# Moving the rounded operands of a hybrid DeltaNet/MoBA block to other addresses in SBUF

## The reference, cut to what matters

```
h = rms_norm(x, norm_pre_w)
proj = h @ w_in                                   # 1024 x 10256
qkv_a, z_a, beta_a, dec_a, qkv_b, z_b, gate_logits = split(proj)
oa = gated_delta_rule(conv+silu+l2norm of qkv_a, beta, g)     # 8 heads of 128, chunks of 64
ya = rms_norm(oa, dn_onorm_w) * silu(z_a)
ob = moba_attention(qkv_b, rel_bias)              # 8 heads of 128; one block of 256: causal attention with a bias
yb = ob * silu(z_b)
gates = sigmoid(gate_logits + b_gate)             # two branches
merged = gates[0] * (ya @ w_branch[0]) + gates[1] * (yb @ w_branch[1])
out = x + rms_norm(merged @ w_out, norm_post_w)
```

## Time and profile before

| | |
|---|---|
| median of 3 runs | 357.66 us |
| the profiled execution | 357.55 us |
| its span (first to last instruction) | 355.8 us |
| TensorE matmuls busy | 347.6 us (98%), 2387 records |
| TensorE weight loads busy | 318.4 us (89%) |
| VectorE busy | 270.0 us (76%) |
| ScalarE busy | 218.8 us (62%) |
| GpSimd busy | 58.7 us (16%) |
| moved by DMA | 63.48 MB, mean 178 GB/s |
| granted clock of TensorE | 0.998 |

### The profile page before, as it was taken

One profiled execution on the slowest core, in us unless ns is written; L12 is line 12 of the kernel. 1 busy time (PEld: TensorE's weight loads), 2 busy tenths in 40 slices (PEclk: granted clock), 3 DMA queues, 4 the chain that ended last, 5 costly groups with the idle time before them and its releaser, 6 DMA issues.

```text
span 355.8 us, 6674 instructions
## 1 busy us (share of the span) xinstructions
PE 347.6 (98%) x2387; PEld 318.4 (89%) x2387; DVE 270.0 (76%) x551; ACT 218.8 (62%) x483; POOL 58.7 (16%) x114
## 2 busy tenths in 40 slices
PE   7999999999999999999999999999999999999993
PEld 5889998888899999999999999999998888888882
DVE  3869897599997868978788797878977656566744
ACT  5877894542457667686867766777676544425421
POOL 1534436500050000301103020030301101000011
PEclk9999999999999999999999999999999999999999
DMA  8667948793698485446745565465534735766423
GB/s 264 178 193 194 334 158 270 198 329 119 167 257 228 121 214 141 121 122 164 188 120 128 145 178 147 120 164 145 165 121 138 247 118 172 254 226 236 124 113 118
DMA packets 76206, 63.48 MB, mean 178 GB/s; under 512 B 4724, under 2 KB 62478, under 8 KB 76174
## 3 DMA queue, kind: packets, MB, share of 16 engines
q1 hardware_dynamic: 73838, 59.37, 57.3%
q0 software_dynamic: 1152, 3.30, 3.1%
q10 hardware_dynamic: 1184, 0.39, 0.5%
HBM read 61.46 MB, written 1.59 MB: 177 GB/s over the span
## 4 chain that ended last, share of the span: by engine, by line
PE 84%; DVE 8%; DMA 3%; issue 2%; ACT 1%; POOL 0%; DVEq 0%; SPq 0%; ACTq 0%; POOLq 0%
PE banks L1395 40%; PE banks L1450 15%; PE banks L1657 6%; PE banks L1413 6%; DVE w_lo L919 3%; DVE sub L1061 2%; DMA xin<-in_x_dram 1%; DMA raw<-in_w_in_dram 1%; DMA sub<-m_blocks 1%; PE banks L1545 1%; PE banks L1523 1%; PE banks L1562 1%; PE banks L1551 1%; PE banks L1380 1%; DVE sub L1063 1%
## 5 line engine op out<-in xcount | busy, mean ns | idle before, releaser
L919 DVE TENSOR_TENSOR w_lo<-raw,w_hi 128x1024 fp32r<-128x1024 f32 x102 | 123.8, 1220 | 42.3 <-ACT w_hi L670 41.6
L670 ACT CAST w_hi<-raw 128x1024 fp32r<-128x1024 f32 x103 | 107.2, 1047 | 30.0 <-PE banks L1450 12.3
L1395 PE MATMUL banks<-h_hi,w_hi 128*128 128x256 f32 x440 | 64.0, 288 | 0.2 <-DVE acc L989 0.2
L1395 PE MATMUL banks<-h_lo,w_hi 128*128 128x256 f32 x440 | 59.4, 277 | 0.0
L1395 PE MATMUL banks<-h_hi,w_lo 128*128 128x256 f32 x440 | 59.3, 277 | 0.0
L1395 PEld LDWEIGHTS banks<-h_hi,w_hi 128*128 128x128 f32 x440 | 55.2, 189 | 0.7 <-DVE acc L989 0.3
L1395 PEld LDWEIGHTS banks<-h_hi,w_lo 128*128 128x128 f32 x440 | 54.2, 188 | 0.0
L1395 PEld LDWEIGHTS banks<-h_lo,w_hi 128*128 128x128 f32 x440 | 54.2, 188 | 0.0
L989 DVE SCALAR_TENSOR_TENSOR acc<-banks,vec,acc 128x255 f32<-128x255 f32 (+2 forms) x72 | 34.5, 480 | 3.7 <-ACT acc L790 1.5
L616 POOL TENSOR_TENSOR so<-so,rnq 128x2 f32<-128x2 f32 x8 | 2.0, 251 | 162.8 <-ACT junk L857 162.8
L790 ACT ACTIVATE acc<-banks,vec 128x256 f32<-128x256 f32 x16 | 7.6, 473 | 17.4 <-PE banks L1395 17.4
(11 more groups left out here) (258 smaller groups left out, 607.6 us busy)
## 6 DMA issues: line engine op xcount, KB each, us to landing
raw<-in_w_in_dram SPq DMA_DIRECT2D x80, 512.0 KB, 4.9
raw<-in_w_branch_dram SPq DMA_DIRECT2D x16, 512.0 KB, 4.7
raw<-in_w_out_dram SPq DMA_DIRECT2D x8, 512.0 KB, 4.2
xin<-in_x_dram SPq DMA_DIRECT2D x2, 512.0 KB, 3.8
th_E<-g_rows POOLq DMA_DIRECT2D x2, 512.0 KB, 7.2
bias<-bias_rows POOLq DMA_DIRECT2D x1, 1024.0 KB, 7.5
raw<-in_x_dram SPq DMA_DIRECT2D x2, 512.0 KB, 3.7
out_dram<-xin SPq DMA_DIRECT2D x4, 256.0 KB, 2.0
```

What stands on the lines that cost most here:

```text
L670: nc.scalar.copy(w_hi[:, t % SLOTS, :], raw[:, t % SLOTS, :]).then_inc(s_hi, 1)
L919: v.tensor_tensor(w_lo[:, t % SLOTS, cols], raw[:, t % SLOTS, cols], w_hi[:, t % SLOTS, cols].bitcast(F32), ALU.subtract).then_inc(s_lo, 1)
L1395: last = mm(ps, w, r, start=part == 0 and k == 0, stop=part == 2 and k == KT - 1)
```

## The change

The declarations are put into another order. Nothing else changes: every instruction, its operands' names and shapes, and every wait are the same, and so is the order of the instructions on each of the five engines.

```diff
@@ build @@
+        gt = sb("gt", [P, 12, NC, HEADS])
+        wbd2 = sb("wbd2", [P, KT, 4 * HEADS], F32R)
+        ssqk = sb("ssqk", [P, NC, HEADS])
+        ng = sb("ng", [P, NC, HEADS])
         raw = sb("raw", [P, SLOTS, D])
         w_hi = sb("w_hi", [P, SLOTS, D], F32R)
         w_lo = sb("w_lo", [P, SLOTS, D], F32R)
+        bd_lo = sb("bd_lo", [P, NC, 2 * HEADS])
+        bd = sb("bd", [P, NC, 2 * HEADS])
+        h_hi = sb("h_hi", [P, KT, SEQ], F32R)
+        h_lo = sb("h_lo", [P, KT, SEQ], F32R)
+        y_hi = sb("y_hi", [P, 2, HEADS, SEQ], F32R)
+        y_lo = sb("y_lo", [P, 2, HEADS, SEQ], F32R)
         xin = sb("xin", [P, NC, D])
...
-        wbd2 = sb("wbd2", [P, KT, 4 * HEADS], F32R)
-        bd_lo = sb("bd_lo", [P, NC, 2 * HEADS])
...
-        h_hi = sb("h_hi", [P, KT, SEQ], F32R)
-        h_lo = sb("h_lo", [P, KT, SEQ], F32R)
...
-        bd = sb("bd", [P, NC, 2 * HEADS])
-        gt = sb("gt", [P, 12, NC, HEADS])
...
-        ng = sb("ng", [P, NC, HEADS])
...
-        ssqk = sb("ssqk", [P, NC, HEADS])
...
-        y_hi = sb("y_hi", [P, 2, HEADS, SEQ], F32R)
-        y_lo = sb("y_lo", [P, 2, HEADS, SEQ], F32R)
```

## The result

The changed kernel takes **363.06 us**, the median of 4 runs (362.92 to 363.44), against 357.60 (357.46 to 357.78) of the kernel before on the same chip: a ratio of 1.0154, interval 1.0136 to 1.0172. It is slower by 5.5 us, outside the range that was given.

A forecast was written before the change was run, and what follows sets the result against it. TensorE was taken to bound the kernel, time being matmul count times pitch. Gains of 1.3 (wide), 0.3 (narrow) and 0.1 (loads) made 1.7 us, giving 356.0 us; range 351.5 to 361.5, the forecast's own 354.5 to 357.2.

The forecast's parts named there:

- where the weights begin, where h and y begin: Rounded matmuls on TensorE: new start addresses hold the pitch at 113.1 ns per 256 columns, gaining 1.3 + 0.3 us.
- best end: Rounded matmuls: pitch falls towards the full clock, 106.7 ns for 256 columns, but not below the weight load, 110.
- worst end: Rounded matmuls: the slow pitch already seen in some narrow tiles, 117.5 ns per 256 columns, holds everywhere.
- The narrow part: Q/K/gate tiles streaming 256 columns: 17 slow groups of 8 matmuls, 0.63 us in all, half taken as gain, 0.3 us.
- The wide part: Gate, branch and output tiles streaming 512 columns: 432 matmuls outside the 41 us stretch gain 3 ns each, 1.3 us.
- Loads: DMA landings of raw and x: the better-aligned start gains 0.1 us, bounds 0 and 0.8 us.
- the count of beats: 512-byte load at offset 128: 20 beats for 16, so a fifth of the landing's transfer part, at most 0.8 us, would go.
- ScalarE and VectorE: Casts, subtractions, heads, substitution and softmax keep their relative addresses: no gain, no loss.
- Tile entry: First matmul of a tile, often followed only after 200 ns because of semaphore waits: unchanged, nothing taken.
- The stretch of 41 us: 64.9 to 105.9, set by loads, VectorE and casts: shorter pitch becomes idle, longer counts almost in full; TensorE slack 0.15 us.
- The slower one: Rival, every rounded matmul: reads agreeing modulo 256 make the slow pitch the rule, +10.6 us, 368.3; chance 0.24.
- The one for no effect: Argument for the no-effect rival (357.7 us, chance 0.26): h and y, 256 bytes apart, give 229.2 and 229.6 ns.

The follow-up runs named there:

- before_y: Kernel before with 64 bytes put ahead of y_hi, so y lies at the same place modulo 256 as the weights; 357.52 us against 357.74.
- two_starts: Kernel before with w_hi and w_lo slots 256 bytes longer and weights of all wide tiles 192 bytes into their slot; 357.39 us against 357.50.
- narrow64: Changed kernel with w_hi and w_lo slots 256 bytes longer and weights of narrow tiles 64 bytes into their slot; 357.56 us against 357.74.
- gap448: Changed kernel with 192 bytes put between the weights and h, weights left at a multiple of 2048; 358.44 us, ratio 1.0021.

## Why the prediction was wrong

The forecast was 356.0 us, a gain of 1.7; the kernel lost 5.5.

*The step that failed* is the term "where the weights begin, where h and y begin". Between a best end of 110 ns and a worst end of 117.5, it took "the best column rate already seen, 113.1 per 256, held throughout". It measured 120.0, beyond the worst end, which had been taken from the slow thirds as if nothing could be slower. The reason given, that "113 is what both kinds of stationary width reach", read 113 as a property of the stream. It was a property of the stream at a distance of 192, which all its rows shared, L1337 too (h 320 - 128 for `wbd2`).

*The narrow part*: forecast 0.3 us less, measured 6.4 more. *The wide part*: forecast 3 ns for each of 432 matmuls, 1.3 us; the mechanism was right, 227.5 and 226.7 in the chain; the size was 1.2 ns for L1450 on average, since behind a tile's entry some matmuls take 231 to 236, and 0.7 us in all. *Loads*: 0.1 us forecast, 0.1 per landing measured, off the chain now; the fifth of a landing that the count of beats allowed, at most 0.8 us, did not show. *ScalarE and VectorE*: no change, right. *Tile entry*: still 200 ns in the changed kernel, right.

*The stretch of 41 us*: that a longer pitch there counts almost in full was right; the chain stays on TensorE through it.

*The rivals.* The slower one, with a chance of 0.24, was right that two reads disturb each other by their starts modulo 256 and that every narrow tile would be slow. But it made agreement the cause, and the table shows that agreement is not special for narrow tiles: at 96 and 208 they are as slow as at 0 (119.8, 118.2 to 119.3), and it is 192 that stands out. For the wide ones it had the sign wrong, as agreement is their best place. Its full price of +10.6 was twice what was measured, since half of it was for the wide ones. That its narrow share, 5.5 us, equals the measured total is luck: it took 117.5 ns where 120.0 came, and the narrow ones cost 6.4, of which the wide ones gave back 0.7. Two arguments carried the wrong weight. The one against it, "the slow pitch appears today without that coincidence", mistook a second phase at the good distance for the whole effect. The one for no effect was sound as far as it went: h and y are 256 bytes apart and equal, and the distance indeed counts modulo 256. But the change moved the other part of the address, and the text said itself that no pair of that kind existed. With no row at such a distance and two pitches already unexplained, an equal weight on both sides of zero would have been the honest reading.

By the rule of the Trainium skill ("SBUF — State Buffer", Who interferes with whom) TensorE never waits on anyone and its two read ports are independent. The first half, which is about other engines, was not tested. The runs disagree with the second: the same stream takes 113.3 or 120.0 ns by the distance to the weights that are loaded beside it, and 116.5 on average when that load has 32 columns in place of 128.

*What stays open*: what decides between the fast and the slow phase at the distance of 192. Five kernels have it with 23, 24 and 38 slow thirds where the weights lie 128 behind a multiple of 256 (kernel before, before_y, two_starts), 59 where they lie 64 behind (narrow64) and 71 where they lie at the multiple (gap448). The phase isn't random: in the last two the same tiles are slow, from the third head on two of the six of each head in all three thirds (n = 41, 47, ... 71 and 43, 49, ... 73), which are fast or slow in the first third alone in the kernel before. So place and order of tiles count there, and no run separates them. Open too is by what arrangement of the memory 192 is good when narrow operands are streamed and 0 when wide ones are. Nothing was run on the second beyond the table.

## What to carry to other kernels

Where rounded float32 matmuls stand back to back, measure the distance between starts for each kind, and look at the difference of the two operands' addresses modulo 256, not at round numbers: here it was worth 6% of a 256-column matmul, and 16 bytes cost more than half of that. A tensor declared at the top of a program moves every tensor behind it, so an edit that seems to touch nothing can cost as much as this one; keep the distance when adding tables, or scan it with one kernel whose slots begin at different places. Check before aligning something whether the present layout is already at a good distance.

## What the runs showed of the hardware

- A rounded matmul of 256 columns has a best pitch of 113.3 ns (272 cycles of 2.4 GHz), one of 512 columns 226.7 (544): 17 cycles for 16 columns. The first was seen at the distance of 192, with weights 32 or 128 columns wide, the second at 0. Plain float32 takes 215 to 219 ns per record of 256 columns, 1 to 3% over 512 cycles, where the rounded ones are 6% over one cycle for a column.
- A stream and the weight load beside it disturb each other, by the difference of their addresses modulo 256: at a difference of 0 the pitch is unchanged when both move by 128 (119.6) or one by 256 (119.6).
- The pitch is again regular at distance 0 (120.0 ns, 288 cycles, in whole thirds) and the weight load is 3 to 4 ns longer (191 and 192 for 188).
- At the good narrow distance there is a second, slower phase of 117.5 ns, which mostly holds for whole tiles, in 23 to 71 of 165 thirds by the layout.
